# Dilated attention of a two-block transformer: queries and keys projected by token block, 512 columns a head, with 32 features turned there

## The reference

```
def _partial_rotary(x, pos):              # x[..., 128]; only the first 32 features turn
    rot = x.shape[-1] // ROPE_FRACTION    # 32
    half = rot // 2                       # 16
    inv_freq = ROPE_THETA_2 ** (-jnp.arange(half, dtype=jnp.float32) / half)
    ang = pos.astype(jnp.float32)[:, None] * inv_freq[None, :]
    ...
    x1, x2, rest = x[..., :half], x[..., half:rot], x[..., rot:]
    return jnp.concatenate([x1 * cos - x2 * sin, x2 * cos + x1 * sin, rest], axis=-1)

def _dilated_mixer(x, w_in, w_out, pos):
    z = x @ w_in                          # 256 x 1024 @ 1024 x 5120
    q = z[..., :3072]  as (3 groups, 8 heads, 256, 128);  k, v = the rest as (8, 256, 128)
    q = _partial_rotary(q, pos);  k = _partial_rotary(k, pos)
    for g in 3 groups:  o_g, lse_g = attention with the causal mask of dilation 1, 4 or 16
    o = sum over g of softmax(lse)_g * o_g
    return o @ w_out
```

## Time and profile before

| | us |
|---|---|
| median of 3 runs | 1760.89 |
| lowest, highest | 1757.55, 1763.1 |
| the profiled execution's own time | 1762.83 |
| its span in the profile | 1761.0 |
| PE busy in the span | 1674.4 |
| DVE busy | 1139.6 |
| ACT busy | 918.2 |
| POOL busy | 311.1 |

### The profile page before, as it was taken

One profiled execution on the slowest core, in us unless ns is written; L12 is line 12 of the kernel. 1 busy time (PEld: TensorE's weight loads), 2 busy tenths in 40 slices (PEclk: granted clock), 3 DMA queues, 4 the chain that ended last, 5 costly groups with the idle time before them and its releaser, 6 DMA issues.

```text
span 1761.0 us, 29911 instructions
## 1 busy us (share of the span) xinstructions
PE 1674.4 (95%) x12408; PEld 1515.2 (86%) x12408; DVE 1139.6 (65%) x1824; ACT 918.2 (52%) x1449; POOL 311.1 (18%) x228
## 2 busy tenths in 40 slices
PE   6999999999999999999999998889999899889998
PEld 5889998999888899989998887768888789868886
DVE  4465656687555565557874677668844777779844
ACT  4646855566446468556663564335633455445631
POOL 0000021144000000302440052114500200006400
PEclk9999999999999999999999999999999999999999
DMA  6524345465555243454546532115565344235652
GB/s 202 181 64 162 115 149 198 148 209 174 189 173 151 92 141 118 167 192 166 194 168 206 205 130 96 52 49 192 191 217 189 145 144 144 96 120 191 232 198 72
DMA packets 45543, 274.03 MB, mean 156 GB/s; under 512 B 4704, under 2 KB 8928, under 8 KB 16352
## 3 DMA queue, kind: packets, MB, share of 16 engines
q1 hardware_dynamic: 44688, 267.41, 44.3%
q10 hardware_dynamic: 720, 4.72, 0.8%
HBM read 271.06 MB, written 1.05 MB: 155 GB/s over the span
## 4 chain that ended last, share of the span: by engine, by line
PE 79%; DVE 10%; ACT 4%; issue 3%; DMA 3%; POOL 0%; SPq 0%; DVEq 0%; ACTq 0%; POOLq 0%
PE b_ps L354 11%; PE b_ps L356 11%; PE b_ps L357 11%; PE b_ps L456 9%; PE b_ps L457 8%; PE b_ps L459 8%; PE b_ps L400 6%; DVE b_wlo L311 3%; PE b_ps L401 3%; DMA b_wraw<-in_w 2%; PE b_ps L977 2%; ACT b_S L929 1%; PE b_ps L956 1%; PE b_ps L1866 1%; PE b_ps L1082 1%
## 5 line engine op out<-in xcount | busy, mean ns | idle before, releaser
L311 DVE TENSOR_TENSOR b_wlo<-b_wraw,b_whi 128x2048 fp32r<-128x2048 f32 (+2 forms) x266 | 577.5, 2175 | 195.0 <-PE b_ps L459 128.2
L303 ACT ACTIVATE b_whi<-b_wraw 128x2048 fp32r<-128x2048 f32 (+2 forms) x266 | 470.9, 1772 | 218.4 <-PE b_ps L459 150.2
L354 PE MATMUL b_ps<-b_H,b_whi 128*128 128x256 f32 x1784 | 520.4, 292 | 8.2 <-ACT b_zrot L807 5.1
L356 PE MATMUL b_ps<-b_H,b_whi 128*128 128x256 f32 x1784 | 506.8, 284 | 0.0
L357 PE MATMUL b_ps<-b_H,b_wlo 128*128 128x256 f32 x1784 | 506.6, 284 | 0.0
L354 PEld LDWEIGHTS b_ps<-b_H,b_whi 128*128 128x128 f32 x1784 | 344.2, 193 | 17.9 <-issue 7.1
L356 PEld LDWEIGHTS b_ps<-b_H,b_whi 128*128 128x128 f32 x1784 | 344.3, 193 | 1.5
L357 PEld LDWEIGHTS b_ps<-b_H,b_wlo 128*128 128x128 f32 x1784 | 344.0, 193 | 0.0
L400 PE MATMUL b_ps<-b_H,b_whi 128*128 128x512 f32 x448 | 157.2, 397 | 0.0
L1435 POOL TENSOR_TENSOR b_fl<-b_ab,b_fh 128x256 fp32r<-128x256 f32 x44 | 93.8, 2132 | 226.6 <-ACT b_fh L1408 226.6
L401 PE MATMUL b_ps<-b_H,b_wlo 128*128 128x256 f32 x448 | 125.0, 279 | 0.0
(11 more groups left out here) (359 smaller groups left out, 2923.3 us busy)
## 6 DMA issues: line engine op xcount, KB each, us to landing
b_wraw<-in_w SPq DMA_DIRECT2D x223, 1024.0 KB, 4.9
b_wraw<-in_w SPq DMA_DIRECT2D x39, 512.0 KB, 3.7
b_bias<-in_rpb SPq DMA_DIRECT2D x8, 512.0 KB, 11.1
b_gains<-in_gains ACTq DMA_DIRECT2D x4, 1024.0 KB, 5.1
b_wraw<-in_w SPq DMA_DIRECT2D x2, 768.0 KB, 4.2
b_cA<-in_cA SPq DMA_DIRECT2D x2, 576.0 KB, 7.7
b_X<-in_x SPq DMA_DIRECT2D x2, 512.0 KB, 4.6
out<-b_X SPq DMA_DIRECT2D x4, 256.0 KB, 2.6
```

The source lines that it names most:

```text
L303: e.activation(whi[u % NHI][:, 0:n], raw[u % NRAW][:, 0:n], ACT.Copy).then_inc(up("w_hi", "whi", u))
L311: e.tensor_tensor(wlo[u % NLO][:, 0:n], raw[u % NRAW][:, 0:n], hi.bitcast(F32), ALU.subtract).then_inc(up("w_lo", "wlo", u))
L354: e.matmul(out, wh, x.hi[:, kk, :], start=k == 0, stop=False)
L356: e.matmul(out, wh, x.lo[:, kk, :], start=False, stop=False)
```

## The change

The queries and keys of a head are now made like the values: token block still, 512 weight columns (the three queries and the key of the head) streaming. The result lies with tokens on partitions. ACT copies it to `b_rot`, two buffers, one for each token block. DVE turns only the first 32 features of each of the four vectors, in four short operations. PE then transposes the four 128x128 pieces back to features on partitions, into banks 2 and 7, and ACT copies them to `b_diQK`. The query factor moves into the masked minimum, as its scale of minus 128^-0.5 with masks of minus 1e30. Four pieces n = 0 to 3 are now a head: unit 0 at token block 0, unit 0 at block 1, unit 1 at block 0, unit 1 at block 1. ACT and DVE split one unit each at n = 0 and at n = 2. POOL's four gain operations stand ahead of the additions of heads 0 to 3, one each. The two units of the second value set stand at the end of `fill`.

```diff
+    class Turned:
+        def __init__(self, ctx, table, need):
+            self.rows, self.table, self.need, self.parts = sb(ctx, "rot", [P, 2, 512]), table, need, scr[0:2]
+    def turned_copy_act(e, w, tn, job, j, tb, old):
+        if old is not None:
+            w.wait_ge(*at("full", ("back", *old, tb)))
+        row_act(e, w, job, j, tb, tn.rows[:, tb, :])
+    def turned_dve(e, w, tn, job, j, tb):
...
+        w.wait_ge(*at("free", (job.key, j, tb)))
+        e.tensor_tensor(t1[:, :, 0:16], v[:, :, 16:32], sn[:, :, 0:16], ALU.mult)
+        e.tensor_tensor(t1[:, :, 16:32], v[:, :, 0:16], sn[:, :, 16:32], ALU.mult)
+        e.tensor_tensor(t0, v[:, :, 0:32], cs, ALU.mult).then_inc(up("rot_parts", "rot_parts", job.key, j, tb))
+        w.wait_ge(*at("rot_parts", job.key, j, tb))
+        e.tensor_tensor(v[:, :, 0:32], t0, t1, ALU.add).then_inc(up("rot_rows", "rot_rows", job.key, j, tb))
+    def turned_pe(e, w, tn, job, j, tb, ring):
+        bank = banks.take(w, ("back", job.key, j, tb), ring)
+        w.wait_ge(*at("rot_rows", job.key, j, tb))
+        for g in range(4):
+            ins = e.transpose(bank[:, g * P:g * P + P], tn.rows[:, tb, g * P:g * P + P], ident)
+        ins.then_inc(banks.full(("back", job.key, j, tb)))
+    def turned_act(e, w, job, j, tb, dst):
...
+        e.activation(dst, banks.tile(key)[:, :].rearrange("p (g t) -> p g t", g=4), ACT.Copy).then_inc(banks.free(key))
...
-            fill = [("qk", (0, j)) for j in range(16)] + [("qend", (0,)), ("v", (0,)), ("v", (1,))]
-            fill += [("qk", (1, j)) for j in range(16)] + [("qend", (1,))]
-            due = [7, 11, 15, 20, 26, 30, 34, 36]
+            self.blocks = [(pi, tb) for pi in range(2) for tb in range(2)]
+            fill = [("qk", (h, n)) for h in range(8) for n in range(4)] + [("v", (0,)), ("v", (1,))]
+            due = [6, 10, 14, 18, 22, 26, 30, 34]
...
+        def qk_pe(self, e, w, h, n):
+            row_pe(e, w, self.qk[h // 4], h % 4, *self.blocks[n])
+            if n == 3:
+                turned_pe(e, w, self.tn, self.qk[h // 4], h % 4, 0, "back")
+            elif n == 0 and h:
+                self.last_pe(e, w, h - 1)
+        def last_pe(self, e, w, h):
+            turned_pe(e, w, self.tn, self.qk[h // 4], h % 4, 1, "back")
+        def qk_act(self, e, w, h, n):
+            if n % 2 == 0:
+                ahead_to(e, w, split_hi, begun[(self.qk[h // 4].key, h % 4)][n // 2] + AHEAD_HI)
+            if n == 2:
+                self.copy_act(e, w, h, 0)
+            elif n == 3:
+                self.copy_act(e, w, h, 1)
+                self.back_act(e, w, h, 0)
+            elif n == 0 and h:
+                self.back_act(e, w, h - 1, 1)
+        def qk_dve(self, e, w, h, n):
+            if n % 2 == 0:
+                ahead_to(e, w, split_lo, begun[(self.qk[h // 4].key, h % 4)][n // 2] + AHEAD_LO)
+            if n >= 2:
+                turned_dve(e, w, self.tn, self.qk[h // 4], h % 4, n - 2)
...
-            banks.assign(lin=SOME, att=ATT)
+            banks.assign(lin=[0, 1], back=[2, STAT], att=ATT)
...
         def pool(self, e, w):
-            for tb in range(2):
-                w.wait_ge(*at("full", (self.qk[0].key, 2 + tb)))
-                for plus in range(2):
-                    gains_pool(e, w, "l20", 2, tb, plus)
             for what, i in self.steps:
                 if what == "scores":
+                    if i[0] < 4:
+                        w.wait_ge(*at("full", ("back", self.qk[0].key, i[0], 1)))
+                        gains_pool(e, w, "l20", 2, i[0] // 2, i[0] % 2)
                     scores_pool(e, w, self.att, *i)
```

More of the change, by code:

```diff
@@ L55, in shape_constants, with turns, both @@
     c["cos2"], c["sin2"], c["perm2"] = rope(128, 32, 500000.0, 128)
-    def both(ok):
-        m = np.where(ok, 0.0, BIG)
+    def turns(dim, rot, theta):
+        half = rot // 2
+        inv = np.float32(theta) ** (-np.arange(half, dtype=np.float32) / np.float32(half))
+        ang = tok.astype(np.float32)[:, None] * inv.astype(np.float32)[None, :]
+        cs, sn = np.cos(ang), np.sin(ang)
+        by_tok = np.concatenate([cs, cs, -sn, sn], axis=1)
+        return np.concatenate([by_tok[0:P], by_tok[P:T]], axis=1)
+    c["turns2"] = turns(128, 32, 500000.0)
+    def both(ok, far=BIG):
+        m = np.where(ok, 0.0, far)
         return np.concatenate([m[0:P], m[P:T]], axis=1)
@@ L834, in turn_dve @@
         sig.same(("rotated", job.key, j), ("turned", tn.key, n))
+    class Turned:
[6 more added lines that the diff above has]
+    def turned_dve(e, w, tn, job, j, tb):
+        v = tn.rows[:, tb, :].rearrange("p (g c) -> p g c", g=4)
+        t0, t1 = (tn.parts[tb][:, P * i:P * i + P].rearrange("p (g c) -> p g c", g=4) for i in range(2))
+        cs, sn = (tn.table[:, 64 * tb + a:64 * tb + a + 32].unsqueeze(1).broadcast_to([P, 4, 32]) for a in (0, 32))
+        w.wait_ge(*at(*tn.need))
+        w.wait_ge(*at("free", (job.key, j, tb)))
[11 more added lines that the diff above has]
+    def turned_act(e, w, job, j, tb, dst):
+        key = ("back", job.key, j, tb)
+        w.wait_ge(*at("full", key))
+        e.activation(dst, banks.tile(key)[:, :].rearrange("p (g t) -> p g t", g=4), ACT.Copy).then_inc(banks.free(key))
     class Attn:
@@ L2330, in __init__, with qk @@
                 hg, h = h8 // 4, h8 % 4
[L2331 to L2335, removed]
+                QK, V = self.sets[hg]
+                def qk(e, ps, g, QK=QK, h=h):
+                    e.matmul(ps[:, 0:P], QK[:, h, g, 0:P], QK[:, h, 3, 0:P], start=True, stop=True)
+                    return e.matmul(ps[:, P:P + T], QK[:, h, g, P:T], QK[:, h, 3, :], start=True, stop=True)
                 heads.append(head(qk=[lambda e, ps, g=g, qk=qk: qk(e, ps, g) for g in range(3)],
-                                  masks=[[CD(f"dil{g}")[:, 0:P], CD(f"dil{g}")[:, T:2 * T]] for g in range(3)], widths=[P, T],
-                                  needs=[("rotated", f"diqk{hg}", 4 * h + 3)], tables=[("cD",)], d=P,
+                                  masks=[[CD(f"dil{g}")[:, 0:P], CD(f"dil{g}")[:, T:2 * T]] for g in range(3)], widths=[P, T], scale=-(128.0 ** -0.5),
+                                  needs=[("free", ("back", f"diqk{hg}", h, tb)) for tb in range(2)], tables=[("cD",)], d=P,
                                   v=lambda kb, h=h, V=V: V[:, kb, P * h:P * h + P], vneeds=[("free", (f"div{hg}", 0, tb)) for tb in range(2)], out=(self.y, h8)))
             self.att = Attn("dil", heads, S_ring, T_ring, small)
-            fill = [("qk", (0, j)) for j in range(16)] + [("qend", (0,)), ("v", (0,)), ("v", (1,))]
-            fill += [("qk", (1, j)) for j in range(16)] + [("qend", (1,))]
-            due = [7, 11, 15, 20, 26, 30, 34, 36]
+            self.blocks = [(pi, tb) for pi in range(2) for tb in range(2)]
+            fill = [("qk", (h, n)) for h in range(8) for n in range(4)] + [("v", (0,)), ("v", (1,))]
+            due = [6, 10, 14, 18, 22, 26, 30, 34]
             made, wo = due[0], 0
@@ L2369, in pe @@
             first_rows_pe(e, w, self.v[0], "l20", "ln")
-            banks.assign(lin=SOME, att=ATT)
+            banks.assign(lin=[0, 1], back=[2, STAT], att=ATT)
             for what, i in self.steps:
                 if what == "qk":
-                    rot_pe(e, w, self.qk[i[0]], i[1], self.tn)
+                    self.qk_pe(e, w, *i)
                 elif what == "v":
[L2375 to L2378, removed]
+                    for tb in range(2):
+                        row_pe(e, w, self.v[1], 0, i[0], tb)
+                    if i[0] == 0:
+                        self.last_pe(e, w, 7)
                 elif what == "scores":
@@ L2391, in act @@
         def act(self, e, w):
-            first_rows_act(e, w, self.v[0], self.sets[0][2])
+            first_rows_act(e, w, self.v[0], self.sets[0][1])
             for what, i in self.steps:
                 if what == "qk":
-                    rot_act(e, w, self.qk[i[0]], i[1], self.tn)
+                    self.qk_act(e, w, *i)
                 elif what == "v":
-                    tb, = i
-                    ahead_act(e, w, self.v[1], 0)
-                    row_act(e, w, self.v[1], 0, tb, self.sets[1][2][:, tb, :])
+                    ahead_to(e, w, split_hi, begun[(self.v[1].key, 0)][i[0]] + AHEAD_HI)
+                    if i[0] == 0:
+                        self.back_act(e, w, 7, 1)
+                    else:
+                        for tb in range(2):
+                            row_act(e, w, self.v[1], 0, tb, self.sets[1][1][:, tb, :])
                 elif what == "scores":
@@ L2426, in dve @@
                 if what == "qk":
-                    rot_dve(e, w, self.qk[i[0]], i[1], self.tn, self.place(i[0]))
+                    self.qk_dve(e, w, *i)
                 elif what == "v":
-                    ahead_dve(e, w, self.v[1], 0)
-                elif what == "qend":
-                    turn_dve(e, w, self.qk[i[0]], 15, self.tn, self.place(i[0]))
```

(1 more changed line is left out.)

30 lines of the change are left out of this document (14 added, 16 removed).

## The result

| | us |
|---|---|
| before, median of 8 runs beside it | 1761.22 (1756.83 to 1767.3) |
| changed, median of 8 runs | 1772.98 (1767.53 to 1872.99) |
| ratio, 95% interval | 1.0055 (1.0036 to 1.0075) |
| forecast | 1773.4 (1757 to 1786) |

The account below looks back on a forecast made before the run. PE, busy 95% of the span, was taken to bound the kernel. The terms -11.8 - 13.6 - 4.9 + 31.6 + 11.2 = +12.5 us on the profiled 1762.8 give 1775.3, less 1.9 for the median: 1773.4 (1757 to 1786).

Parts of the forecast that it names:

- PE's own stream: On PE, projection 5.0 us shorter, 13.8 us of permutations gone, 7.0 us of transposes added: -11.8 us.
- part 2: PE's old waits for copy, permutation and rotation go, 13.6 us, and 4.9 us of half-clock loss with them.
- Old stops and their clock: PE's waits for copy, permutation and rotation vanish, -13.6 us, with the half-clock loss behind them, -4.9 us.
- New stops: PE waits before block 0's transposes for DVE's turning: 3.9 us at heads 2 to 7, +31.6 us over eight heads.
- Head 1: PE's new stop at head 1, following the first exponentials with a 1.3 us table load in front: 5.2 us.
- Head 0: PE's new stop at head 0, where ACT's copy stands behind a split with a late load: taken as 3.0 us.
- The clock: Half clock on PE behind the new stops: 1.4 us at each of 8, +11.2 us, bounds 0 and 23.
- POOL's gains: POOL's gain operations, now one a head, cost nothing; at most 6 us at four heads if their cover is gone.
- Rival B: PE's new stops come but the clock stays high: +1.3 us, 1762; chance 0.17.
- C: DVE turns early enough, so only head 0's stop and its clock loss remain: -25.9 us, 1735; chance 0.14.
- D: POOL's gain operations lose their cover and every stop costs 2.9 us of clock: about 1791; chance 0.09.
- The point at which the forecast would turn over: The result turns over where seven PE stops with their clock loss fall below about 26 us, 3.7 each.

Follow-up runs that it names:

- e5: e4 with each of the 64 transposes of the dilated stage made twice into the same place: 1741.18 us, ratio 0.9871.
- e6: The kernel before with each of the 32 permutation products of the dilated stage made twice: 1767.15 us, ratio 1.0031.
- e4: The changed kernel with both blocks' transposes behind the next head's first piece and the second unit split behind both turnings: 1731.91 us, ratio 0.983.
- e1: The changed kernel again, no edit, for a second profile: 1774.62 us, ratio 1.0064.
- e3: The changed kernel with 14 unused 128x512 matmuls ahead of block 0's transposes at each head: 1757.87 us, ratio 0.9973.
- e2: The changed kernel with DVE turning a head's block 0 before, not after, the second unit's split: 1741.0 us, ratio 0.9883.
- e8: e4 with POOL's four gain operations put back ahead of the first scores, as in the kernel before: 1736.72 us, ratio 0.9857.
- e7: e4 with the split of the head's second unit back ahead of the turning, as in the changed kernel: 1737.23 us, ratio 0.9849.

## Why the prediction was right, step by step

- **PE's own stream** (forecast -11.8). In the changed kernel the score-free pieces run 128x512 at 0.227 us (24 starts from 1505.29 to 1510.71, the first 0.2 slower), as in the earlier trace rows. A transpose costs 0.109 (e5) and a permutation 0.44 (e6). Together with part 2 the terms come to -27.2 in e4, against -27.4 measured.
- **Old stops and their clock** (-13.6, -4.9). Gone. The second was a little small: the kernel before ran at half clock until 1401.7 and 1538.3 us, so for 10.7 us of work and not 9.8, which is 5.3.
- **New stops** (+31.6). Measured 27.6 in the profile's waits, plus 0.16 each, because the profile counts from the end of a 0.39 us matmul and the forecast from its 0.23 slot: 28.9. Heads 2 to 7 stop 3.72 in place of 3.9. In the rows above the split ends at 1433.01 and the rotation at 1433.81: turning takes 0.80 us in place of 0.9, so the guess between its bounds (0.64 and 1.7) was good and 0.1 high. PE starts 0.05 behind it in place of 0.14.
- **Head 1** is where a link was wrong: 3.57 + 0.16 = 3.7, not 5.2. The forecast put ACT's table load of 1.3 us in front of the exponentials. It ran while ACT had nothing to do, before DVE's minima were there:

```profile
1400.98 0.60 ACT L879 ACTIVATE b_diQK<-b_ps 128x512 f32<-128x512 f32 x1 [1.60 <-PE b_ps L873]
1401.60 1.28 ACT L974 ACT_TABLE_LOAD   x1
```

- **Head 0** (3.0): 2.69 + 0.16. ACT's split waited 3.29 us for its weights (3.12 in the earlier trace rows).
- **The clock** (+11.2, bounds 0 and 23). Measured 13.95 as e1 minus e3, 14.2 with head 0's overshoot, 1.8 a stop and not 1.4. By stop it was uneven. The cycles from one stop to the next, less those of e2 lengthened by the longer stop (2.14 us), leave 1.3, 1.6, 2.6, 2.8, 2.7, 0.0 and 1.6. Behind the last stop the way to the end of the stretch, compared with e2's, leaves 1.7. The sum is 14.3. The low level lasted some 6.8 us at heads 2, 3 and 4, where it began 0.9 to 1.2 us before PE resumed, and 3.4 us at heads 0, 1, 6 and 7. The stop at 1496.06 was as long as its neighbours and cost nothing.
- **POOL's gains** (0). In the changed kernel no turning is slowed. e8 shows, in e4's order, that this was worth 4.3 us: in front, they blocked the new turnings.
- **Sum.** -11.8 - 13.6 - 4.9 + 28.9 + 14.2 = +12.8, measured +11.8. The forecast's +12.5 was right in each sign and in its mechanism. Two of its sizes were off, stops 2.7 too much and clock 3.0 too little, and they cancelled: that the total came out within 1 us was in part luck. The sum also counts the new stops from PE's slot and the old ones from the end of a matmul. By my estimate the seven old waits are 0.16 us longer each when counted alike, 14.7 in all. With that and the 5.3 the sum is +11.3, and e4's is -28.1 against -27.4: the terms close to about 0.7 us, not to 0.2.

Rival B (no clock loss) falls by e3, C (DVE in time) by the 27.6 us of waits, and D by the undisturbed turnings and by 1.8 a stop, not 2.9. The point at which the forecast would turn over (26 us of stops and clock at seven heads) agrees with the runs on either side of it, though none lies near it. The seven stops of e2 come to 10 us without clock loss, and it is faster by 0.9 to 1.5%; those of the changed kernel come to 26 us and 13 of clock, and it is slower.

What stays open: why one of seven equal stops was not followed by the low clock. The idle time in front of them differs by 0.02 us. No run varied what decides it, and with the one profile of the changed kernel shown here it is not known whether the same stop goes free in another execution.

## What to carry to other kernels

Where a change puts a new wait on the engine that bounds the stage, follow one period on both engines and look for the longest thing in front of the releasing operation that nobody needs yet. Here it was a 2.3 us split, and moving it alone was worth 29.5 us in the stage (34 by the medians). Price a stop of TensorE by its length and by the slow clock behind it: here the 1.42 us stops were free of it and the seven 3.56 us stops cost another 1.8 on average. Compare close variants by the length of the stage between two landmarks, because the time in front of it varied by up to 8 us, and the edits of e5, e7 and e8 moved the stage by 2.5 to 6.3.

## What the runs showed of the hardware that I had not expected

- Useless matmuls in a stop made the kernel faster: 112 of 128x512 in place of 25 of the 27.6 us of waits gave 14 us of clock back (0.91 to 1.00 in the stretch).
- Stops of 3.56 us were followed by up to 2.8 us of loss in one place and by none in another, in one execution.
- POOL beside DVE stretched a 0.22 us operation to 2.42 us. Each lost the rest of the POOL operation that it ran into, so the short ones lost most in proportion: 2 elements took 0.88 us in place of 0.16, 64 elements up to 2.42 in place of 0.22.
- ACT loaded its table, 1.28 us, ahead of any use, while it waited for the operation's input.
